# A diffusion backbone step on one core: the first shift and scale in quarters beside three input blocks, one quad of modulation products moved to the output projection

## The reference, cut to what matters

```python
mp = jnp.split(jax.nn.silu(c_ctx) @ ada_w[l] + ada_b[l], 6, axis=-1)   # 6 x 1024: shift, scale, gate, shift, scale, gate
ms = [m[:, None, :] for m in jnp.split(jax.nn.silu(c) @ ada_w[l] + ada_b[l], 6, axis=-1)]
h = x * (1 + scale) + shift
gate_b, gate_c, u, q, k, v, g_conv, g_attn = jnp.split(h @ w_in_l, IN_SPLITS, axis=-1)
# short convolution; differential attention; sigmoid gates; merged @ w_out_l
# LayerNorm, then SwiGLU (layer 0) or top-2-of-8 experts (layer 1), LayerNorm
```

## Time and profile before

| what | value |
|---|---|
| three runs | 1148.20, 1150.58, 1150.67 us |
| median | 1150.58 us |
| the profiled execution, its own time | 1150.42 us |
| its span in the profile | 1148.6 us |
| PE busy | 1122.9 us of the span, 98% |
| DVE, ACT, POOL busy | 866.9, 693.1, 110.4 us |
| moved by DMA | 335.74 MB, mean 292 GB/s |

### The profile page before, as it was taken

How to read it: one execution, slowest core, us unless ns; L and a number is a source line. 1 busy time by engine, 2 the same in 40 slices (tenths; PEclk the granted TensorE clock), 3 DMA queues, 4 the chain that set the end, 5 groups by cost and what they waited for, 6 DMA issues and landing times.

```text
span 1148.6 us, 15666 instructions
## 1 busy us (share of the span) xinstructions
PE 1122.9 (98%) x5553; PEld 892.7 (78%) x5553; DVE 866.9 (75%) x1236; ACT 693.1 (60%) x1010; POOL 110.4 (10%) x131
## 2 busy tenths in 40 slices
PE   5999999999999999999999999999999999999998
PEld 1666667888689889767777888888888888888885
DVE  1766657767775455588767776789999999998997
ACT  2544445644744344464545654678887888878884
POOL 4230100000061000031010000011011010000010
PEclk9999999999999999999999999999999999999999
DMA  9999887656749946597676466389999999999991
GB/s 352 354 376 353 301 326 258 210 191 230 279 160 401 345 149 203 181 329 256 211 237 213 151 222 224 137 317 360 390 381 403 367 409 400 390 403 375 382 401 67
DMA packets 139418, 335.74 MB, mean 292 GB/s; under 512 B 6705, under 2 KB 27297, under 8 KB 139361
## 3 DMA queue, kind: packets, MB, share of 16 engines
q1 hardware_dynamic: 130784, 307.25, 73.7%
q0 software_dynamic: 8544, 27.73, 6.9%
q10 hardware_dynamic: 32, 0.01, 0.0%
HBM read 317.63 MB, written 17.33 MB: 292 GB/s over the span
## 4 chain that ended last, share of the span: by engine, by line
PE 87%; DVE 7%; DMA 3%; ACT 1%; issue 1%; SPq 1%; DVEq 0%; ACTq 0%
PE bank L1440 25%; PE bank L1442 25%; PE bank L1441 25%; DVE w_lo L903 3%; DMA raw<-in_ada_w 3%; PE bank L1664 3%; PE bank L1729 1%; PE bank L1747 1%; PE bank L1609 1%; PE bank L1737 1%; PE bank L1598 1%; ACT w_hi L586 1%; SPq L348 1%; PE bank L1558 0%; PE bank L1537 0%
## 5 line engine op out<-in xcount | busy, mean ns | idle before, releaser
L903 DVE TENSOR_TENSOR w_lo<-raw,w_hi 128x1024 fp32r<-128x1024 f32 (+1 forms) x504 | 593.1, 1205 | 174.7 <-ACT w_hi L586 169.7
L586 ACT ACTIVATE w_hi<-raw 128x1024 fp32r<-128x1024 f32 (+1 forms) x504 | 503.5, 1009 | 317.8 <-PE bank L1442 301.5
L1440 PE MATMUL bank<-w_hi,xT_hi 128*128 128x512 f32 (+1 forms) x1056 | 411.8, 390 | 4.0 <-DVE w_lo L903 2.6
L1442 PE MATMUL bank<-w_lo,xT_hi 128*128 128x512 f32 (+1 forms) x1056 | 402.2, 381 | 0.0
L1441 PE MATMUL bank<-w_hi,xT_lo 128*128 128x512 f32 (+1 forms) x1056 | 401.4, 380 | 0.0
L1440 PEld LDWEIGHTS bank<-w_hi,xT_hi 128*128 128x128 f32 x1056 | 199.6, 189 | 47.4 <-DVE w_lo L903 7.4
L1442 PEld LDWEIGHTS bank<-w_lo,xT_hi 128*128 128x128 f32 x1056 | 198.4, 188 | 35.4
L1441 PEld LDWEIGHTS bank<-w_hi,xT_lo 128*128 128x128 f32 x1056 | 199.0, 188 | 30.9
L1440 PE MATMUL bank<-w_hi,hT_hi 128*128 128x512 f32 x360 | 142.7, 396 | 0.1
L1442 PE MATMUL bank<-w_lo,hT_hi 128*128 128x512 f32 x360 | 140.5, 390 | 0.0
L1441 PE MATMUL bank<-w_hi,hT_lo 128*128 128x512 f32 x360 | 140.3, 390 | 0.0
(11 more groups left out here) (256 smaller groups left out, 829.0 us busy)
## 6 DMA issues: line engine op xcount, KB each, us to landing
raw<-in_w_in SPq DMA_DIRECT2D x52, 1024.0 KB, 6.6
raw<-in_ada_w SPq DMA_DIRECT2D x48, 1024.0 KB, 9.7
raw<-in_moe_w_down SPq DMA_DIRECT2D x40, 1024.0 KB, 8.4
raw<-in_moe_w_gate SPq DMA_DIRECT2D x32, 1024.0 KB, 7.5
raw<-in_moe_w_up SPq DMA_DIRECT2D x32, 1024.0 KB, 7.0
raw<-in_moe_w_gate SPq DMA_DIRECT2D x16, 768.0 KB, 9.9
raw<-in_moe_w_up SPq DMA_DIRECT2D x16, 768.0 KB, 8.9
raw<-in_w_attn_out SPq DMA_DIRECT2D x8, 1024.0 KB, 5.1
```

The source lines that it names most:

```text
L586: nc.scalar.activation(w_hi[:, unit, 0:n], raw[:, r, at:at + n], ACT.Copy).then_inc(hi_done, 1)
L903: V.tensor_tensor(w_lo[:, unit, 0:n], raw[:, r, at:at + n], w_hi[:, unit, 0:n].bitcast(F32), ALU.subtract).then_inc(lo_done, 1)
L1440: pe.matmul(o, hi, wh, start=start, stop=False)
L1442: return pe.matmul(o, hi, wl, start=False, stop=stop)
```

## The change

- Quad 0 becomes four *quarters* (`FIRST = 4`). Quarter i is columns 256 i to 256 i + 255 of both the shift and the scale, over all 1024 rows: two halves of 1 MiB, now of 1024 rows by 256 columns (rows of 1 KB instead of 2 KB in memory). A quarter gives the coefficients for 256 channels, which is one unit's depth.
- The first three input blocks (`FIRST_POS = 3`) are multiplied unit by unit side by side: unit 0 of blocks 0, 1, 2, then unit 1 of the three, and so on, 12 units in four rounds. Block 2 gets banks 4 and 5. Each unit has a transfer of its own (0.5 MiB).
- Three halves (both of quarter 1, the first of quarter 2) land in parts of `work` outside the ring, which are free at that time.
- SP, not POOL, loads the tokens, first of all. ACT loads the bias and `ln_in` weights; the LayerNorm of group 1's tokens runs on DVE; DVE also copies the transposed tokens out of PSUM and makes the residual `x` (`first_x`, four operations of 128x1024), which POOL did.
- Quad 3 moves out of the input blocks: its four pairs of halves stand in the output projection (`out_pair`), its turn before the last row block. The eight pairs of quads 1 and 2 come at every third tick from 12 on. Attention jobs in layer 0 begin at tick 12.
- The transposes of the output projection use banks 0 and 1 alone, in both layers. The third and fourth portion wait for the splits of the first two (`oT_ok`).

```diff
-GROUPS = [(4 * i, 4 * i + 4) for i in range(4)] + [(16, 18), (18, 20), (20, 24)]
+FIRST = 4
+FIRST_POS = 3
+GROUPS = [(i, i + 1) for i in range(FIRST)] + [(4 * i, 4 * i + 4) for i in range(1, 4)] + [(16, 18), (18, 20), (20, 24)]
...
-        STEP0 = 2 * PARTS + 2
+        STEP0 = (FIRST_POS * PARTS, 2 * PARTS + 2)
...
-        PAIRS_AT = ((5, 8, 10, 13, 16, 18, 21, 24, 26, 29, 32, 34), (6, 14, 22, 30))
+        PAIRS_AT = (tuple(range(12, 36, 3)), (6, 14, 22, 30))
+        OUT_PAIRS_AT = (1, 1, 2, 1)
...
-        stream = [("ada", n // 2, n % 2) for n in range(2 * QUAD)]
+        early = both(1) + [("ada", 2, 0)]
+        stream = both(0) + three(0) + [("ada", 2, 1)] + three(1) + both(3)
...
+            for g, name in enumerate(("x_prompt", "x_sample")):
+                sp.dma_start(x[:, g, :], a[name][0]).then_inc(ld_x[g], 16)
+            for unit in range(PARTS):
+                fill_first(unit)
+                for pos in range(FIRST_POS):
+                    fill_unit(pos, unit)
...
+            for i in range(FIRST):
+                ada_copy(i)
+                for n in ((0,), (3, 4), (6, 7), (9, 10))[i]:
+                    first_unit_hi(n)
+                first_modulated(i)
+                for n in ((1, 2), (5,), (8,), (11,))[i]:
+                    first_unit_hi(n)
...
+            def first_halves(i):
+
+                at, w = G * (QUAD - 1 - i), COL // 2
+                for half in range(2):
+                    tile, landed, count = first_home(i, half)
+                    if i and half == 0:
+                        pe.wait_ge(ada_out, i)
+                    pe.wait_ge(landed, count)
+                    for k in range(KD):
+                        j = k % 4
+                        ins = pe.matmul(bank[ADA][32 * j:32 * j + 32, half * w:(half + 1) * w], cond_st[:, k, at:at + 32],
+                                        tile[:, k * w:(k + 1) * w], start=k < 4, stop=k >= 4)
+                    ins.then_inc(ada_sum, 1)
...
-            for n in range(6, 8):
-                ada_half(n)
             pe.wait_ge(idle_zero, 1)
-            idle_products(3, 7)
-            ada_turn(0, bank[2][:, :])
-            idle_products(16, 7)
+            ada_turn(0, first_cols)
+            idle_products(6, 7)
+            for n in range(FIRST_UNITS):
+                pos, unit = first_unit(n)
+                first_multiplied(n)
+                if n == FIRST_POS:
+                    pe.wait_ge(ld_vec, 16 * N_VEC)
+                    pe.transpose(bank[2][:, P:2 * P], vec_rows, ident[:, :]).then_inc(vec_t, 1)
+                if unit < FIRST - 1:
+                    if pos == 0:
+                        first_halves(unit + 1)
+                    if pos == 1:
+                        if unit == 1:
+                            pe.wait_ge(vec_ok, 1)
+                        ada_turn(unit + 1, first_cols)
...
+                pe.wait_ge(oT_ok, 4 * l + 2)
                 turn_heads((2, 3))
-                pe.wait_ge(oT_ok, 4 * l + 2)
                 pe.wait_ge(conv_out, 2 * l + 1)
```

More of the change, by code:

```diff
@@ L294, in program @@
                 stream += [("weights", d, half) for d in range(Q_LAYER * SLOTS, turn0[1] * SLOTS) for half in range(2)]
+                stream += [("none", i, 0) for i in range(len(early))]
         place = {entry: i for i, entry in enumerate(stream)}
@@ new lines, in first_modulated @@
+            def first_modulated(i):
+                ks = slice(2 * i, 2 * i + 2)
+                act.wait_ge(first_coef, i + 1)
+                act.wait_ge(turned_kept, 2 * G)
+                for k in range(2 * i, 2 * i + 2):
+                    ins = nc.scalar.activation(modulated[:, 0, k, :], modulated[:, 0, k, :], ACT.Identity,
+                                               bias=modB[:, 0, k, 0:1], scale=modA[:, 0, k, 0:1])
+                ins.then_inc(first_act, 1)
+                for g, done in enumerate((first_act, first_dve)):
+                    act.wait_ge(done, i + 1)
+                    nc.scalar.activation(xT_hi[:, ks, g, :], modulated[:, g, ks, :], ACT.Copy).then_inc(first_hi, 1)
@@ new lines, in _ @@
+            scales(0, 0)
+            then(V.bn_stats(st[:, 1, 1, :], x[:, 1, COL:2 * COL]))
+            V.bn_aggr(mv[:, 1, :], st[:, 1, :, :].rearrange("p a b -> p (a b)")).then_inc(stats_ok, 1)
+            scales(0, 1)
+            dve.wait_ge(nmr_ok, G)
+            dve.wait_ge(xhat_ok, 2)
+            for half in range(2):
+                at = slice(half * COL, (half + 1) * COL)
+                V.tensor_scalar(xhat_at[0][:, 1, at], x[:, 1, at], rstd[:, 1:2], nmr[:, 1:2], ALU.mult, ALU.add).then_inc(xhat_ok, 1)
@@ L1224, in _ @@
             dve.wait_ge(vec_t, 1)
-            V.tensor_copy(vecT[:, :], bank[6][:, 0:P]).then_inc(vec_ok, 1)
             then(V.tensor_copy(biasT[:, :], bank[6][:, P:2 * P]))
-            dve.wait_ge(ada_cols, 1)
-            ada_keep(0, bank[2][:, :])
+            for g in range(G):
+                for half in range(2):
+                    dve.wait_ge(xhat_t, 2 * g + half + 1)
+                    V.tensor_copy(modulated[:, g, 4 * half:4 * half + 4, :], four(bank[4 * g + half])).then_inc(turned_kept, 1)
@@ L1387, in _ @@
                 coefficients(2 * l + 1)
-                if l == 0:
-                    coefficients(2)
                 def merge(half):
```

443 lines of the change are left out of this document (295 added, 148 removed).

## The result

The changed kernel takes **1152.45 us** in the median of 10 runs (1150.58 to 1156.39), the kernel before on the same chip 1149.85 us (10 runs, 1147.98 to 1152.59). The ratio, taken over the single runs, is 1.0029, with a 95% interval of 1.0018 to 1.0040: 0.3% slower, where 1139.3 us were forecast. Its profiled execution took 1150.64 us with a span of 1148.7 us, as good as equal to that of before (1148.6).

The account below looks back on a forecast made before the run. PE was taken as the bound, busy 1122.9 of 1148.6 us. A gain of 13.1 by tick 12, less 1.0 for late DMA and 1.0 behind tick 12, gave 11.1 off 1150.4: 1139.3 us, range 1134 to 1147.

Parts of the forecast that it names:

- the stretch from tick 20 to the experts the same length as before plus one turn less: Sign of a right forecast: behind the input blocks' early ticks nothing lengthens, up to the experts; no us given.
- Rival E: Something unseen holds ticks 12 to 16 for ten us, giving back the whole early start: 1150 us, chance 0.04.
- Rival C: Quarter loads: a 1 KB piece takes as long as a 2 KB one, 19.8 us lost: 1158.1 us, chance 0.05.
- The first product: Start of the input blocks: first product at 19.5 us, against 35.19 before.
- A quarter's products: In the four rounds: 16 products of 256 columns take 1.9 us, bounds 1.85 and 3.7.
- Rival A: Start and rounds: narrow quarters cost as much per product as wide ones, 7.5 us lost: 1146.8 us, chance 0.09.
- DMA in the rounds: Quarters of 1 KB rows in the four rounds: the last lands late, PE loses 1.0 us.
- e: Extra DMA time per quarter from 1 KB rows: between 0 and 2.9 us, taken as 0.7.
- B: Rival on quarter loads: 1 KB rows cost 2.9 us more per quarter, 9.8 us lost: 1148.1 us, chance 0.08.
- Tick 12: Input blocks, 49th group of products, three blocks done: starts at 61.0 us, against 80.4 before.
- rival D: Rounds: order binds through late ln_in loads, some 5 us lost, 1144 us, or the clock falls; chance 0.12.
- What is owed, and the output projection: 6.3 us of pairs and job 0 still owed at tick 12; quad 3 costs PE the same in either place.

Follow-up runs that it names:

- the last experiment: Kernel with seats spread, quad 3 back between input blocks, eighteen idle products; second group's residual steps moved to tick 13, lambda's to 11, 12, 13: 1145.64 us, 0.9964 of kernel before.

## Why the prediction was wrong

The forecast was 1139.3 us with a range from 1134 to 1147, and 88 in 100 for faster. It was slower by 0.29%.

**The step that failed** is the last one of what would show it right, "the stretch from tick 20 to the experts the same length as before plus one turn less", and with it the silent assumption of the sum that whatever is gained at tick 20 reaches the end. The sum priced the start, the rounds, the ticks behind them and the output projection, and took all behind as unchanged. But the change also edits the list that SP follows at the end of the feed-forward stage, and that edit was given no price, not even nothing with a cover named. The trace of before would have warned: the first load of layer 1's weights was issued at 473.85, landed at 478.86 and was taken up at 483.41, with 4.6 us to spare. In the place of "the same length" the runs showed that the three empty seats make this load land 11.4 us later (483.65 against 472.21 with the seats spread), of which 4.6 were covered, and that they cost 6.5 us from unit 120 to the end, in the changed kernel and in the kernel before alike. The experiment that gives the seats alone to the kernel before measured 5.5 us of whole span.

None of the rivals was this. Rival E, "the early start is given back whole", named the size (1150) and the wrong place (tick 12 to 16), at 0.04; that its size came out is luck. Rival C, the slower one, rested on dear 1 KB rows and has fallen.

**The terms of the sum, one by one.**

*The first product* was forecast at 19.5 and stood at 18.88: right.

*A quarter's products*: 1.9 us were forecast from bounds of 1.85 and 3.7, and 1.86 were measured. Rival A has fallen: strip products of 256 columns take half the time of those of 512.

*DMA in the rounds*: 1.0 us was priced for quarters of 1 KB rows that come late. No quarter was late. From 18 to 20 us nothing but such rows moves, from 22 to 24 nearly nothing but 2 KB rows:

```profile
DMA packets 700, 0.70 MB, mean 350 GB/s; under 512 B 16, under 2 KB 700, under 8 KB 700
```

```profile
DMA packets 393, 0.77 MB, mean 384 GB/s; under 512 B 18, under 2 KB 18, under 8 KB 393
```

A MiB is 3.00 against 2.73 us, and a quarter has two, so that e = 0.54. The 0.7 that were taken were near; the 2.9 of the line through the earlier trace rows were not, and B and C have fallen. That line took the mean of the 1.5 KB rows, 79 ns a packet by the trace's own packets, with ramps in it: their median is 65 ns, beside 88 for 2 KB, and for 1 KB it is 51 from 18 to 20 us of the changed kernel. The estimate from the Trainium skill's "DMA: Bandwidth & Descriptors", Why small descriptors are slow, that was set beside it had 4.5% more for 1 KB pieces, e = 0.25, and no loss. This trace shows 10% more, twice as much, and bears out that nothing was lost.

*Tick 12* was forecast at 61.0 and stood at 65.44. Of these 4.4 us, 1.7 are the low clock behind the first product (19.48 to 22.90, 3.4 us at half rate) and 1.7 the wait for DVE's copies. In the kernel that had neither (DVE relieved) the way from the first product to unit 12 was 43.07 us, 1.6 more than the forecast 41.5, against a first product that came 0.6 earlier in the changed kernel: 1.7 + 1.7 + 1.6 - 0.6 is the whole. This part was rival D in kind, the order and the clock, and its price for one fall of the clock, 1.8, was right. Its signs were not: DVE waited only 0.6 us for an `ln_in` load, and what made tick 12 late was its copies behind the residual's steps and lambda's loads; and the granted clock was 0.96 from 20 to 60 us, not below 0.95.

*What is owed, and the output projection*: forecast as even. The quad costs 8.74 us where it stands now and 8.01 between the blocks. At the end of the output projection 11.1 us were forecast and 6.34 measured. Tick 12 came 4.4 us too late, the 1.0 for DMA in the rounds was not lost, and behind tick 12 the lead of 14.98 us shrank by 8.6 instead of the 6.3 owed and 1.0 lost: 1.3 more, 0.7 of them the dearer quad. Together that is 4.7 of the 4.8 that were missing; the unpriced seats then took all that was left.

*A stall's cover*: the experiments show one thing about these 4.4 us that the sum did not have. From 61 to 81 us DMA is full, and a wait taken from PE there comes back as a wait for DMA. Tick 12 came 1.7 us earlier there, and tick 16 came no earlier. That kernel has a pair at every second tick. In the changed kernel's own order, a pair at every third, eighteen idle products brought unit 12 0.72 us earlier and unit 16 0.49, so how much of the 4.4 us would last there is not shown.

**The rest of the difference.** The two profiled spans agree to 0.1 us, but the medians differ by 2.6. The changed kernel's ten runs have mean clocks of 0.991 to 0.996; the four from 1153.87 to 1156.39 us are those with 0.991 or 0.992. The kernel before had 0.995 to 1.000 in the 80 runs beside the experiments. With the seats spread, and nothing else, the clock is 0.998 or 0.999 in six of six, and with eighteen idle products besides it goes down to 0.995. So the long wait also brings low clock behind it. Part of that is in the profile: 0.89 from 470 to 500 us, with the transposes at 1.97 instead of 1.36 us. The first product behind them stands 1.4 us later than before, and that is made good by 500 us, where both traces stand level. As an estimate, 0.005 less of mean clock over 1150 us is 5.7 us, enough for what the slower four runs took beyond the profiled one (3.2 to 5.8 us), but where in the program their clock fell is in no profile that was taken. The fall near 735 us that some of the other kernels' traces show (below) is a candidate, and was not shown to be it.

## What to carry to other kernels

A load queue of fixed seats turns an edit of its order at one end of the program into a change of lead at the other: of each entry added or dropped, count how many loads fewer stand ahead of the next stage's first weights, and look in the trace for how long that stage's first load had been there before it was used (here 4.6 us, less than the 5.7 that the first empty seat took). Where a dummy entry is needed, put it where transfers have time to spare, not at a border between stages, where an engine's next work stands behind the first load. And a gain at the start counts only when it has been followed to the last instruction of the list that the change touches.

## What the runs showed of the hardware

Four small loads slowed a whole core. Where lambda's loads moved to 15 us (each a row of 256 B, broadcast to 128 partitions through POOL's queue, 64 packets of 2 KB in all), the rate of the core fell to 149 GB/s for 4 us. The 61 packets in that window took 0.63 us of an engine each, while 490 packets of the other queue took 58 ns each (44.4% of 16 x 4 us). By the trace's packets, 32 of the 61 are lambda's, at 1.2 us in the mean and 2.9 at most; the other 32 of the same loads, from 19.2 to 19.9 us, took 0.09 us each. At their usual place, from 50 to 56 us of the changed kernel, where two other small loads of POOL's stand beside them, the rate falls to 155 GB/s as well, shortly before the stretch in which DMA is full. The broadcast as such is not shown to be the cause: the input norm's two loads, also broadcast through POOL's queue, are 256 packets of 4 KB from 41 to 46 us of the changed kernel, at 0.17 us each, twice the time of a 2 KB packet of SP's queue. What makes lambda's dear stays open; bringing these vectors in without a broadcast was not tried.

PE's clock did not follow each wait alike. It fell behind idle times of 6.47 us (the changed kernel), 6.36, 6.35, 3.87, 3.61 and 2.54 us, and in the kernel before behind one of 1.62 us, which followed one of 0.63. It did not fall behind the 1.99 and 1.82 us of the last experiment, nor behind the 1.66 us at 65.27 us of the changed kernel. Behind the pause in front of the first product (2.83 us from start to start) it fell in four kernels, and did not in the one with a single seat at the end, whose instructions there are the same. So no length of wait divides the two cases here, and the 3 us assumed before the run with one seat are not borne out. In five of the fourteen traces it also fell once between 732 and 738 us, for 3.4 or 6.8 us, with PE busy around it (16.00 of 16 us in one of them), in kernels with and without the long wait.
